# Four of six adaLN modulation parts beside the compression of the cached keys, two beside the prompt attention

## The reference

```
mod = silu(c) @ w_ada + b_ada            # c: 1 prompt row and 8 sample rows; w_ada 2048 x 12288
shift1, scale1, gate1, shift2, scale2, gate2 = split(mod, 6)
h  = rmsnorm(x) * (1 + scale1) + shift1
p  = h @ w_in                            # queries, keys, values, gates
kvc = compress(cached cmp rows)          # per sample: 2-layer MLP over blocks of 32 rows
m  = mixers(...)                         # prompt attention, then sample attention over caches
x  = x + gate1 * (m @ w_out)
x  = x + gate2 * swiglu(rmsnorm(x) * (1 + scale2) + shift2)
y  = rmsnorm(x)
```

## Time and profile before

| | |
|---|---|
| median of 3 runs | 1987.6 us (1983.35 to 1989.29) |
| the profiled execution, its own time | 1988.14 us |
| its span in the trace | 1986.3 us |
| first stage: first modulation step to first projection matmul | 43.50 to 218.06 us |
| middle stage: first scores to first `turn_keys` | 548.73 to 698.31 us |
| TensorE busy over the span | 1877.6 us (95%) |

### The profile page before, as it was taken

One profiled execution on the slowest core, in us unless ns is written; L12 is line 12 of the kernel. 1 busy time (PEld: TensorE's weight loads), 2 busy tenths in 40 slices (PEclk: granted clock), 3 DMA queues, 4 the chain that ended last, 5 costly groups with the idle time before them and its releaser, 6 DMA issues.

```text
span 1986.3 us, 35820 instructions
## 1 busy us (share of the span) xinstructions
PE 1877.6 (95%) x15449; PEld 1720.4 (87%) x15449; DVE 965.1 (49%) x1552; ACT 750.5 (38%) x1101; POOL 58.6 (3%) x108
## 2 busy tenths in 40 slices
PE   6888999999998878899999989999999999999997
PEld 3555899999954455899999989999999999999996
DVE  3336446554346723544445765444444444654544
ACT  2336433333334532433334334333333333533332
POOL 0000000000000000000000000000000000000000
PEclk9999999999999988799999999999999999999999
DMA  9998388989899946878787976776777676455551
GB/s 367 423 422 319 118 280 281 295 277 286 269 412 417 388 155 234 256 237 262 223 264 238 314 243 209 256 255 232 249 253 258 232 249 231 146 175 180 184 185 47
DMA packets 336261, 512.47 MB, mean 258 GB/s; under 512 B 8882, under 2 KB 310234, under 8 KB 319626
## 3 DMA queue, kind: packets, MB, share of 16 engines
q1 hardware_dynamic: 316162, 368.53, 56.0%
q0 software_dynamic: 5248, 125.73, 15.8%
q10 hardware_dynamic: 14752, 16.80, 3.3%
HBM read 504.29 MB, written 98.91 MB: 304 GB/s over the span
## 4 chain that ended last, share of the span: by engine, by line
PE 85%; DMA 8%; DVE 3%; ACT 2%; issue 1%; SPq 0%; DVEq 0%; ACTq 0%
PE bank L1190 18%; PE bank L1191 18%; PE bank L1192 18%; DMA piece<-in_w_ada 6%; PE bank L869 5%; PE bank L870 5%; PE bank L871 5%; PE bank L750 3%; PE bank L787 2%; DMA mem<-in_cache_sel_kv,runs 1%; PE bank L818 1%; DMA mem<-in_x_sample 1%; PE bank L776 1%; PE bank L1021 1%; PE bank L1089 1%; DMA mem<-in_cache_dil_kv 1%
## 5 line engine op out<-in xcount | busy, mean ns | idle before, releaser
L1190 PE MATMUL bank<-piece,piece 128*128 128x264 f32 x3040 | 865.2, 285 | 5.8 <-ACT piece L1643 5.0
L1191 PE MATMUL bank<-piece,piece 128*128 128x264 f32 x3040 | 865.8, 285 | 0.0
L1192 PE MATMUL bank<-piece,piece 128*128 128x264 f32 x3040 | 864.6, 284 | 0.0
L2168 DVE TENSOR_TENSOR piece<-piece,piece 128x2048 fp32r<-128x2048 f32 (+2 forms) x216 | 441.1, 2054 | 479.5 <-ACT piece L1623 479.5
L1190 PEld LDWEIGHTS bank<-piece,piece 128*128 128x128 f32 x3040 | 573.4, 189 | 6.3 <-ACT piece L1643 5.0
L1623 ACT CAST piece<-piece 128x2048 fp32r<-128x2048 f32 (+2 forms) x216 | 369.0, 1716 | 546.1 <-PE bank L1192 499.3
L1192 PEld LDWEIGHTS bank<-piece,piece 128*128 128x128 f32 x3040 | 573.7, 189 | 0.0
L1191 PEld LDWEIGHTS bank<-piece,piece 128*128 128x128 f32 x3040 | 572.8, 188 | 0.0
L869 PE MATMUL bank<-piece,piece 128*128 128x264 f32 (+1 forms) x816 | 237.9, 292 | 0.0
L870 PE MATMUL bank<-piece,piece 128*128 128x264 f32 (+1 forms) x816 | 232.0, 284 | 0.0
L871 PE MATMUL bank<-piece,piece 128*128 128x264 f32 (+1 forms) x816 | 231.7, 284 | 0.0
(11 more groups left out here) (346 smaller groups left out, 1343.7 us busy)
## 6 DMA issues: line engine op xcount, KB each, us to landing
piece<-in_w_ada SPq DMA_DIRECT2D x48, 2048.0 KB, 12.9
out_s_dil<-in_cache_dil_kv POOLq DMA_DIRECT2D x64, 1023.5 KB, 6.3
piece<-in_w_in SPq DMA_DIRECT2D x50, 1024.0 KB, 8.3
piece<-in_w_gate SPq DMA_DIRECT2D x22, 2048.0 KB, 8.1
piece<-in_w_up SPq DMA_DIRECT2D x22, 2048.0 KB, 8.1
piece<-in_w_down SPq DMA_DIRECT2D x32, 1408.0 KB, 6.5
piece<-in_w_in SPq DMA_DIRECT2D x16, 2048.0 KB, 9.1
piece<-in_w_out SPq DMA_DIRECT2D x8, 2048.0 KB, 9.0
```

The costliest lines, as they stand in the source:

```text
L1190: mm(out, w_high[:, k, :], half_tile(x_high[k]), start=(start and k == first_tile), stop=False)
L1191: mm(out, w_high[:, k, :], half_tile(x_low[k]), start=False, stop=False)
L1192: last = mm(out, w_low[:, k, :], half_tile(x_high[k]), start=False, stop=(stop and k == len(x_high) - 1))
L2168: v.tensor_tensor(half_chunk(a, k_tiles, f, CW), raw, half_chunk(buffer, k_tiles).bitcast(F32), ALU.subtract)\
```

## The change

Part 3 moves from the middle stage into the first: 32 steps run beside the compression (x = 0 to 31) and 16 in the middle, spread over the units 0 to 22. `UNIT_OF_STEP` becomes `i * 22 // 15`, that is the units 0, 1, 2, 4, 5, 7, 8, 10, 11, 13, 14, 16, 17, 19, 20, 22. What follows from the slots changes with it: the loads of chunks 0 and 1 wait for step 30 and those of chunks 2 and 3 for step 31, the first load of the middle goes to slot 2 and so waits for the last projection chunk, and the first projection tile accumulates in bank 7.

```diff
-    ADA_FIRST = 3
+    ADA_FIRST = 4
-        return a % 3 if a < NA1 else (a - NA1) % 3
+        return a % 3 if a < NA1 else (a - NA1 + 2) % 3
     def acc_bank(n):
-        return (1, 3, 0, 2)[n % 4]
+        return (1, 3, 0, 2)[n % 4] if n else 7
-    UNIT_OF_STEP = {NA1 + i: i if i < 2 else i - 1 for i in range(NF)}
+    UNIT_OF_STEP = {NA1 + i: i * (NU - 2) // (NF - 1) for i in range(NF)}
-    TURN_AT = {10: ADA_FIRST, 21: ADA_FIRST + 1, NU + 1: ADA_FIRST + 2}
-    assert max(UNIT_OF_STEP.values()) == NU - 2 and NF == 3 * ADA_STEPS
+    TURN_AT = {12: ADA_FIRST, NU + 1: ADA_FIRST + 1}
+    assert NF == 2 * ADA_STEPS and max(PART_END) == NU - 2 and min(PART_END) <= 10
 (SP, loads of the chunks)
-                sp.wait_ge(*pe_.at("ada", NA1 - 3 if c < 2 else NA1 - 2))
+                sp.wait_ge(*pe_.at("ada", NA1 - 2 if c < 2 else NA1 - 1))
 (SP, loads of the middle)
-            sp.wait_ge(*pe_.at("acc", NT - 2 if a == NA1 else NT - 1))
+            sp.wait_ge(*pe_.at("acc", NT - 2 if a == NA1 + 1 else NT - 1))
-            if a == NA1 + 12:
+            if a == NA1 + 9:
                 sp.wait_ge(*dve_.at("sample_q"))
 (ACT, weights_high)
             if n < 2:
-                act.wait_ge(*pe_.at("ada", NA1 - 1))
+                act.wait_ge(*pe_.at("ada", NA1 - 3))
```

## The result

The changed kernel takes 1989.28 us (median of 20 runs, 1985.85 to 1997.81), the kernel before 1984.30 (20 runs, 1980.55 to 1989.29): a ratio of 1.0026, 95% interval 1.0017 to 1.0034. It is some 5 us slower (3.4 to 6.7 by the interval), inside the 0.3% that the prediction set as no change. The profiled execution of the changed kernel took 1988.64 us, with a span of 1986.8.

The account below looks back on a forecast made before the run. Bounds: TensorE in the projection and from the merge on, DMA in the first four slices and the middle. First-stage loss 19.0 minus middle gain 17.8 (5.6 + 12.2) gives +1.2 us: 1989.3 profiled, 1988.8 median, range 1980 to 1998.

Parts of the forecast that it names:

- First stage: Stage the moved part 3 enters: first projection matmul forecast at 237.1 us against 218.06, a loss of 19.0 us.
- that copy, costed at nothing: ScalarE's copy of part 2 at x = 24: part 3's first step waits for it, hidden by step 26's load wait.
- I take TensorE: First stage, step 30: TensorE's own work of 21 to 22 us between waits sets it, so it starts at 216.5.
- The forecast's other bound: First stage, step 30: four loads at the same rate, 24.8 x 4/5 = 19.8 us, as the alternative to TensorE's work.
- Units 0 to 7: Early middle, paced by TensorE: removed steps of units 1, 3 and 6 gained in full, 5.6 us.
- the first load's later wait is given back: Early middle: first load waits 6.5 us longer, but unit 1's removed step and empty unit 3 return as much.
- Units 8 to 23: Later middle: VectorE binds, its stretch falls from 93.0 to 80.8 us with 1.2 idle, a gain of 12.2.
- the 137 at which I had called this part wrong: Middle, first scores to `turn_keys`: forecast about 132 us instead of 149.6; wrong if it stays above 137.
- Slower by the middle: Rival: TensorE and VectorE hand units to and fro, middle gains 12 us; +7, 1995 us; chance 0.10.
- Faster by the idle tail: Rival: first-stage tail's idle time absorbs added work, loss 9.2; about 1978 us, projection start below about 230; chance 0.10.
- Slower by the old pace: Rival: first stage keeps old pace to step 30, chunks land late, 24.7 lost; 1997 us, start after 242; chance 0.14.

## Why the prediction was right, and where its terms were not

The forecast of 1988.8 us and no change held: 1989.28. That the two are 0.5 us apart is luck. The forecast was a change of +1.2 us on a median of 1987.6; measured are +5.0 on 1984.30. Too little for the change and too much for the start took each other out. In the profiled execution both terms of the sum came out smaller than forecast, the loss by 3.6 us and the gain by 6.8, which leaves +4.4.

**First stage: 19.0 forecast, 15.4 measured.** The mechanism was right: uncovered chunks, then cast, copies, MLP, turn. By its own steps: step 26 was to wait until 194.6; the load did land at 194.76 where TensorE had less to do, but in the changed kernel TensorE got there at 195.57 by itself, having waited 2.55 us for ScalarE's copy of part 2 at step 24. So that copy, costed at nothing, cost up to 0.8. Step 30 came at 214.94 and not at 216.5 (1.6 less), chunk 0 was there 4.1 us after its issue and not 3.2 (0.9 more), chunk 1 3.6 behind it and not 5.6 (2.0 less), and the chain behind took 8.9, not 9.5. "I take TensorE" was right for step 30: TensorE waited for no load from 195 to 220 us. The term was too long, 19.4 us measured for 21 to 22, chiefly because the period before, from which it was read, begins with a step of 3.25 us and this one with 1.93. But the choice decided nothing. The forecast's other bound, four loads in 19.8 us, gives 194.6 + 19.8 = 214.4, and with most of the matmuls gone step 30 came at 214.93. The Trainium skill's fit ("DMA: Bandwidth & Descriptors", section "Anatomy of one DMA") is given for loads that GpSimd issues, and the chunks' loads are SyncE's; by it both chunks were to be there 5.3 us after issue. The trace has 7.7, and 7.6 where nothing stood ahead of them.

**Units 0 to 7: 5.6 forecast, 2.9 in the profile, 4.2 to 4.6 in five other executions.** Here a step was wrong: that the first load's later wait is given back by the removed step of unit 1 and the empty unit 3. The waits of 2.00, 1.04 and 1.90 us stand in units 0 to 2, ahead of the empty one. With the load in its old place the units gained 8.0 to 9.5 us, and the same wait put into the kernel before cost it 6.2, some 1.7 of it by the clock. This line stood at zero in the sum. Another 1.4 to 1.7 us of the profile's miss is the step of unit 2, which ran at the lower clock there (3.58 us) and not in the five.

**Units 8 to 23: 12.2 forecast, 8.1 in the profile, 11.0 to 12.4 where the clock held.** VectorE binds, as said: the forecast had its part at 80.8 us, and it took 80.6 to 80.9 in the seven executions that kept the higher clock in unit 11. The profiled execution lost 3 to 4 us to a fall of the clock there. The sum had no term for the new wait for ScalarE's copy of part 4; the seven have it too (1.73 us), so by itself it costs nothing that shows. Two slips of the working cost nothing either: these units hold ten steps, not eleven, and 16 steps over 22 units of the forecast's 132 us for 24 are one per 7.6 us, not 6.5.

The middle took 138.6 us in the profile, over the 137 at which I had called this part wrong. In the five executions with the same middle stage and the higher clock in units 2 and 11 it took 133.1 to 134.4, against the 132 forecast. There the gain is 15.2 to 16.5 us, about what the first stage loses. That the medians still say +5.0 would fit a clock that falls in many executions: of the 20 runs the ten slower have a median granted clock of 0.972 over the span, the ten quicker 0.9745. That is an indication and not a proof, since no trace shows those stages again.

**The rivals.** Slower by the middle named a gain of 12 us for it; the profile has 11.0, but not for its reason: VectorE's part reached its bound wherever the clock held, and with most of the middle's matmuls gone units 8 to 23 took 86.2 us, where handing to and fro would have shown about 81. Faster by the idle tail asked for a start below 230; even with none of part 3's loads it was 230.6. Slower by the old pace asked for a start after 242, and all four executions with this first stage start before 236.

Settled by runs: the late first load, the cast of chunk 1, and VectorE as the bound of units 8 to 23. In part argued: the two bounds of the tail, since no run leaves out the loads alone. Open: what decides whether the clock falls in units 2 and 11, how often, and so how much of the +5.0 is the clock; and the 3.2 us that the samples' attention was shorter in the profile after, which its spread of nearly 10 us covers.

## What to carry to other kernels

When work is moved into a stretch with spare DMA time, work out when the DMA engines are through with its bytes as well as when TensorE is through with its matmuls: what stands behind both can't start before the later of the two, and if they meet, speeding up one alone gains nothing. Look at the first load behind a stage boundary by itself: here 6.2 us of later issue cost the first units most of that, whatever slack the later units had. And when a cast of a freshly landed buffer stands in an engine's order ahead of copies that another engine waits for, put the copies first once the landing is no longer covered; this and the load's place were worth 0.0044 of the ratio, 8.7 us, more than the whole change moved the time.

## What the runs showed of the hardware that was not expected

The granted clock was not settled by the work just ahead of it. After the same two waits on TensorE in unit 11 (1.28 and 1.73 us) the next step ran at 3.64 us in three executions and at 1.92 in seven, the two levels of 1.2 and 2.4 GHz, and units 8 to 23 took 93.9 to 94.0 against 89.7 to 91.1 us. In unit 2, after the same wait of 1.9 us, it was 3.58 and 3.62 us in two executions and 1.92 in five. These are kernels whose edits lie elsewhere, one profile of each; over the 20 executions of the changed kernel itself the mean granted clock lay between 0.970 and 0.977.

With the DMA engines at their rate, the chunks' loads, issued 3.8 us earlier against TensorE's steps, landed 0.4 us earlier. And with the engines standing still ahead of them, the two chunks (0.39 MB in rows of 192 bytes, 1.05 MB in rows of 512) still took 3.7 and 7.6 us from issue to cast, where 1.44 MB at the 422 GB/s of the modulation loads would be 3.4. Rows of 512 bytes did not reach those 422 either: 302 GB/s in the kernel before, 303 in the changed kernel from 225 to 230 us.
